# A hybrid decoder step: sampling attention with its first loads issued in the phase before, window keys laid in memory order, and the gate products moved in between each unit's keys and values

## The reference, cut to what matters

```python
# A: dilated window attention of the sampling rows over a cache, 3 head groups x 4 heads
sc = einsum('bqhe,bqjhe->bhqj', q, g[:, :, :, 0]) * e ** -0.5     # g: keys gathered by stride
p, den, lse = masked_softmax_parts(sc, valid)
# B: forgetting attention of the sampling rows over paged keys and values, 8 heads, 2048 past rows
s_past = einsum('bqhe,bkhe->bhqk', q, k_past) * e ** -0.5 + cq - c_past
# both row groups: the merge of the branches, gated
mix = (sigmoid(h @ w_ga) * (o_a @ w_pa) + sigmoid(h @ w_gb) * (o_b @ w_pb)) @ w_o
```

## Time and profile before

| | |
|---|---|
| median of 3 runs | 1196.73 us (1194.1 to 1200.82) |
| the profiled execution: its own time, its span | 1199.27 us, 1197.5 us |
| PE busy, DVE busy, ACT busy in the span | 1000.1, 379.9, 206.0 us |
| phase C: first scores to first product of phase D | 397.4 to 794.4 us |
| PE busy in phase C | 323.8 of 397.0 us |
| phase B's second to fifth key loads and last modulation weights: issued from, last weights used | 343.3, 386 us |

### The profile page before, as it was taken

The page is one execution under the profiler, slowest core; times in us unless marked ns, Lnnn a source line. Parts: engine busy times, 40 slices in busy tenths (PEclk is TensorE's granted clock), DMA queues, the critical chain, the costliest instruction groups (busy, mean ns, idle before and its releaser), DMA issues. The chain is left out here.

```text
span 1197.5 us, 17987 instructions
## 1 busy us (share of the span) xinstructions
PE 1000.1 (84%) x7324; PEld 585.3 (49%) x7324; DVE 379.9 (32%) x865; ACT 206.0 (17%) x509; POOL 187.3 (16%) x210
## 2 busy tenths in 40 slices
PE   3999999997897169979989997579977998777770
PEld 2444444444564046647656674136554554444430
DVE  3100033237751164516701771003451222100105
ACT  3000000014542011100020003001231211111114
POOL 0000033311200100022222311100003322212110
PEclk9999999999997589989989998669978999989995
DMA  9976666977787779998969984979187999999966
GB/s 339 355 278 248 249 248 248 326 244 255 256 212 168 207 240 213 289 349 322 370 231 334 364 320 151 391 266 341 57 325 269 364 370 383 379 393 394 397 256 237
DMA packets 98062, 348.48 MB, mean 291 GB/s; under 512 B 13018, under 2 KB 56802, under 8 KB 78654
## 3 DMA queue, kind: packets, MB, share of 16 engines
q1 hardware_dynamic: 80478, 265.90, 64.8%
q0 software_dynamic: 15552, 79.97, 18.1%
q10 hardware_dynamic: 1952, 1.48, 0.5%
HBM read 335.46 MB, written 63.36 MB: 333 GB/s over the span
## 5 line engine op out<-in xcount | busy, mean ns | idle before, releaser
L1605 PE MATMUL bank<-turned,w_all 128*128 128x320 f32 (+1 forms) x512 | 143.7, 425 | 0.0
L442 PE MATMUL bank<-w_all,turned 128*128 128x481 f32 (+2 forms) x384 | 119.3, 503 | 1.1 <-DVE turned L651 1.1
L442 PE MATMUL bank<-w_ring,turned 128*128 128x481 f32 (+2 forms) x384 | 118.4, 502 | 0.0
L2013 PE MATMUL bank<-w_all,mix_row 128*64 128x256 f32 x736 | 92.2, 407 | 26.9 <-DMA w_all<-in_w_exp 25.8
L1605 PEld LDWEIGHTS bank<-turned,w_all 128*128 128x128 f32 x512 | 95.3, 196 | 35.6 <-issue 15.5
L2013 PEld LDWEIGHTS bank<-w_all,mix_row 128*64 128x64 f32 x736 | 60.9, 147 | 65.3 <-issue 46.4
L1709 DVE STREAM_TRANSPOSE mods<-w_all 128x2048 f32<-128x2048 f32 (+1 forms) x39 | 86.6, 2239 | 9.8 <-PE bank L1481 7.1
L442 PEld LDWEIGHTS bank<-w_all,turned 128*128 128x128 f32 (+1 forms) x384 | 56.8, 171 | 61.5 <-issue 58.3
L442 PEld LDWEIGHTS bank<-w_ring,turned 128*128 128x128 f32 (+1 forms) x384 | 57.1, 171 | 60.4 <-issue 57.3
L2059 DVE COPY act_t<-bank 128x128 f32<-128x128 f32 x33 | 9.6, 292 | 200.8 <-PE bank L2023 199.1
L661 DVE COPY w_all<-bank 128x481 f32 (+5 forms) x32 | 16.9, 531 | 152.6 <-PE bank L442 152.4
(11 more groups left out here) (357 smaller groups left out, 1318.5 us busy)
## 6 DMA issues: line engine op xcount, KB each, us to landing
w_all<-in_w_exp SPq DMA_DIRECT2D x22, 2048.0 KB, 41.0
out_a_sample<-in_cache_a SPq DMA_DIRECT2D x8, 4080.0 KB, 21.4
w_all<-in_w_exp SPq DMA_DIRECT2D x25, 1024.0 KB, 39.2
mods<-in_w_ada SPq DMA_DIRECT2D x21, 1024.0 KB, 8.8
w_all<-in_cache_a SPq DMA_DIRECT2D x96, 128.0 KB, 7.5
w_all<-in_cache_a SPq DMA_DIRECT2D x40, 256.0 KB, 6.1
turned<-in_w_exp SPq DMA_DIRECT2D x5, 2048.0 KB, 42.2
mods<-in_w_exp SPq DMA_DIRECT2D x5, 2048.0 KB, 43.7
```

The costliest lines, as they stand in the source:

```text
L442: mm = nc.tensor.matmul(m.banks[i][r:r + ROWS[i], 0:hi - lo], m.hT[:, k, i * P:i * P + ROWS[i]], ring[u][:, CW * k + lo:CW * k + hi], star ...
L1605: mm = nc.tensor.matmul(GATE[:, 0:WIDTH[h]], gate_w[b][k][:, c % 2 * P:(c % 2 + 1) * P], m.hT[:, k, 256 * h:256 * h + WIDTH[h]], start=k = ...
L2013: mm = nc.tensor.matmul(m.banks[2 + p][x * SLOTS:(x + 1) * SLOTS, 0:HID], hgT[:, k, :], m.weights(u)[:, (2 * k + x) * HID:(2 * k + x + 1) ...
```

## The change

It has six parts.

1. Window keys come as one transfer over 128 partitions and 1 KB pieces in memory order (key 4i+c on partition i) where there were four over 32 partitions (key 32c+i): 2 issues in place of 8 for a step, the same bytes and piece size.
2. `add_bias` reads the bank with a stride to put the scores back in key order; for that it takes 256 columns at a time, so a chunk is two operations where it was one.
3. The mask (now built with 128 rows, one transfer), the first gate weights (2 MB) and the first merge weights (0.75 MB) are issued by SP in phase B. The weights lie in slices of 6 rather than 7 per tile, which keeps clear of columns that phase B still reads.
4. The 8 tables of rows are computed by DVE in step 7, not ahead of step 1; the constants are waited for at chunk 3.
5. `TURN = 5` pieces stand in front of the first value step of each unit and `LATE = 2` behind the last key step, so 7 in each handover; the other 52 are spread over steps 1 to 87 at 0.63 per step.
6. ACT takes the tangents of these in the same places, one of them between the two exponentials of kind "b"; the copies of the mixed rows (`LAST_PIECE + 2`) move from step 81 to 89.

```diff
-    for j in range(4):
-        src = I[name][4 * u + j].rearrange("(c i t) n -> i t c n", c=4, t=t)[:, t0:t0 + n, :, 0:AH * HD]
-        dst = slot[32 * j:32 * j + 32, 0:n * 4 * AH * HD].rearrange("p (t c n) -> p t c n", t=n, c=4)
-        for x in range(n):
-            eng.dma_start(dst[:, x], src[:, x]).then_inc(arrived, 16)
+    src = I[name][4 * u:4 * u + 4].rearrange("s (i c t) n -> (s i) t c n", c=4, t=t)[:, t0:t0 + n, :, 0:AH * HD]
+    dst = slot[:, 0:n * 4 * AH * HD].rearrange("p (c t n) -> p t c n", t=n, c=4)
+    for x in range(n):
+        eng.dma_start(dst[:, x], src[:, x]).then_inc(arrived, 16)
...
                 early_keys(k)
                 piece(BEFORE + 1 + k)
+                if k == 2:
+                    sp.dma_start(m.wmask, I["mask_window"]).then_inc(m.mask_in, 16)
+                    sp.wait_ge(turn_a, len(turns))
+                    sp.wait_ge(turn_d, len(turns))
+                    gate_weights_in(sp, I, m, 0, 0)
+                if k == 3:
+                    gate_weights_in(sp, I, m, 0, 1)
+            merge_weights_in(sp, I, m, 0)
...
-    FIRST, END = 3, 80
-    piece_at = {}
-    for n, x in enumerate(pieces):
-        piece_at.setdefault(FIRST + n * (END - FIRST) // len(pieces), []).append(x)
+    LATE, TURN, END = 2, 5, 88
+    first_v = [at[(u, "v", 0)] for u in range(len(UNITS))]
+    rate = (len(pieces) - len(UNITS) * (LATE + TURN)) / (END - 1 - len(UNITS))
+    piece_at, late_at, todo, due = {}, {}, list(pieces), 0.0
+    for t in range(1, N):
+        due += 0 if t in first_v else rate
+        count = TURN if t in first_v else min(int(due + 1e-6), len(todo))
+        due -= 0 if t in first_v else count
+        piece_at[t], todo = todo[:count], todo[count:]
+        if t + 1 in first_v:
+            late_at[t], todo = todo[:LATE], todo[LATE:]
...
-                    cols = slice(512 * c, 512 * c + (512 if c < 3 else P))
-                    ins = add(sc_a[:, cols], S(u, c)[:, 0:cols.stop - cols.start], wmask[:, cols], peak[:, 0, c:c + 1])
+                    dve.wait_ge(m.mask_in, 16)
                     if c == 3:
-                        ins = add(sc_a[:, AT * P:AT * P + GROUPS * NS], S(u, c)[:, P:P + GROUPS * NS], mask_a[:, own(u), :], peak[:, 0, 4:5])
+                        dve.wait_ge(con_in, 16)
+                    for g in (2 * c, 2 * c + 1) if c < 3 else (6,):
+                        lo, w = g % 2 * 256, P if g == 6 else 256
+                        by_key = lambda x: x.rearrange("p (y c) -> p y c", c=4)
+                        ins = add(by_key(sc_a[:, 256 * g:256 * g + w]), S(u, c)[:, lo:lo + w].rearrange("p (c y) -> p y c", c=4),
+                                  by_key(wmask[:, 256 * g:256 * g + w]), peak[:, 0, g:g + 1])
...
-                for x in piece_at.get(t, []):
-                    if x in sums:
-                        gates(*x)
+                now = [x for x in piece_at.get(t, []) if x in sums]
+                for x in now[1:] if t in first_v and kind(STEPS[t][0]) == "b" else now:
+                    gates(*x)
...
             turn(0)
-            dve.wait_ge(pages_in, 16 * 2)
-            for j in range(4):
-                rows = slice(32 * j, 32 * j + 32)
...
-            dve.wait_ge(con_in, 16 * 5)
...
+                    if (u, part, g) == (0, "v", 0):
+                        rows_of_pages()
```

More of the change, by code:

```diff
@@ L129, in build @@
         m.wp_in, m.wo_in = [ctx.enter_context(nc.semaphore(n)) for n in ("w_p", "w_o")]
+        m.gate_in = [ctx.enter_context(nc.semaphore(f"gate_w{b}")) for b in range(2)]
+        m.merge_in, m.mask_in = [ctx.enter_context(nc.semaphore(n)) for n in ("merge_w", "mask_rows")]
         with ExitStack() as attn:
@@ L214, in constants @@
             "over_ids": np.arange(EXPERTS, BLOCKS, dtype=np.float32)[None, :],
-            "mask_window": np.concatenate(window, axis=1), "sample_consts": sample_consts,
+            "mask_window": np.tile(np.concatenate(window, axis=1), (4, 1)), "sample_consts": sample_consts,
             "page_consts": np.concatenate([before, seq_of, tri8], axis=1),
@@ L1177, in phase_c @@
         filled = from_pages if kind(u) == "b" else from_window
-        filled[slot_of[n]] += 16 * (1 if kind(u) == "b" else 8 if part == "k" and g < 6 else 4)
+        filled[slot_of[n]] += 16 * (1 if kind(u) == "b" else 4 if part == "v" else 2 if g < 6 else 1)
         level.append(filled[slot_of[n]])
@@ L1232, in phase_c @@
             pieces += [("gate", c, h, 1, 0), ("gate", c, h, 1, 4), ("out", c, h, 0, 0)]
-    FIRST, END = 3, 80
-    piece_at = {}
-    for n, x in enumerate(pieces):
-        piece_at.setdefault(FIRST + n * (END - FIRST) // len(pieces), []).append(x)
-    step_of = {x: t for t, xs in piece_at.items() for x in xs}
+    LATE, TURN, END = 2, 5, 88
[9 more added lines that the diff above has]
+            late_at[t], todo = todo[:LATE], todo[LATE:]
+    assert not todo
+    step_of = {x: t for xs in (piece_at, late_at) for t, ys in xs.items() for x in ys}
+    LAST_PIECE = max(step_of.values())
     items = [x[1:3] for x in pieces if x[0] == "out"]
@@ L1296, in phase_c @@
         bias_in = [sem(f"bias{x}") for x in range(4)]
-        gate_in, wp_in = [sem(f"gate_w{b}") for b in range(2)], sem("merge_w")
+        gate_in, wp_in = m.gate_in, m.merge_in
         gain_in, terms, terms_out = sem("gains"), sem("terms"), sem("terms_out")
@@ L1617, in _ @@
                     (score if STEPS[t][1] == "k" else weigh)(t)
+                for x in late_at.get(t, []):
+                    piece(*x)
                 for x in use_at.get((t, "after"), []):
@@ L1656, in gates, with exps @@
                 ins.then_inc(th_ok, 1)
-            def exps(u):
+            def exps(u, between):
                 for h in range(1 if kind(u) == "a" else 2):
+                    if h:
+                        for x in between:
+                            gates(*x)
                     e = u if kind(u) == "a" else 2 + 2 * own(u) + h
@@ L1687, in _ @@
                 if t + 1 < N and STEPS[t][1] == "k" and STEPS[t + 1][1] == "v":
-                    exps(STEPS[t][0])
-                if t == max(piece_at) + 2:
+                    for x in late_at[t]:
+                        if x in sums:
+                            gates(*x)
+                    exps(STEPS[t][0], [x for x in piece_at[t + 1] if x in sums][:1])
+                if t == LAST_PIECE + 2:
                     act.wait_ge(mixed, 2 * KD)
@@ L1739, in maxima @@
                 for h in range(1 if kind(u) == "a" else 2):
-                    V.tensor_reduce(nm[:, h:h + 1], peak[:, h, :], AX, ALU.max, negate=True).then_inc(mx, 1)
+                    V.tensor_reduce(nm[:, h:h + 1], peak[:, h, 0:8 if kind(u) == "a" else 5], AX, ALU.max, negate=True).then_inc(mx, 1)
             def recips(u):
@@ L1852, in _ @@
                         recips(u)
+                for x in late_at.get(t, []):
+                    if x[0] == "out":
+                        mixing(*x[1:3])
                 for x in use_at.get((t, "after"), []):
```

60 lines of the change are left out of this document (32 added, 28 removed).

## The result

The changed kernel takes **1164.26 us** in the median of 4 runs (1160.8 to 1167.1), the kernel before 1196.7 beside it: ratio 0.9725, 95% interval 0.9681 to 0.9768. Forecast were 1161 us and 1147 to 1177. The profiled execution took 1167.1 us (span 1165.2), 3 above the median.

What follows compares the result with a forecast made beforehand. Phase C was taken as bound mostly by PE's list of steps and pieces, plus a 27.70 us first stall. Stretches summed to 361.8 against 397.0 us; with 4 gained in phase B and 3 given back, 1161 us, range 1147 to 1177.

Steps and rivals of the forecast that it cites:

- First stretch: Start of phase C: the 27.7 us wait goes, DVE is late next, 48.2 us becomes 20.
- Handovers: From a unit's keys to its values: seven pieces cover the exponentials, with tangent waits 19 us each.
- Key steps: PE waits for DVE, so less is saved than the pieces removed: unit 1 19 us, unit 2 51, unit 3 48.
- unit 3's keys: Key steps of unit 3 in phase C, with two `out` pieces instead of four: 48 us, before 53.2.
- transfers that collide in kind "b": Loads competing from step 28 to 59, 104 us of loads in 115 us: 3 us given back in the sum.
- Tail: Unit 3's values to phase D: 29.3 and 52.7 us; phase D 28 us after w_o goes out, or 38.
- rival (d): End of phase C: w_o load late in full, 10 us, and strided addings cost; 1172 us, chance 0.07.
- Rival (c): DVE keeps ahead of PE in key steps (41.5, not 49) and w_o lands early; 1147 us, chance 0.14.
- Phase B: Faster key loads remove the 4.12 us wait for a modulation weight: 4 us gain, bounds plus 4 and minus 8.
- Rival (b): Key loads stay at 225 GB/s; unit 1's keys and phase B's last weights late; 1176 us, chance 0.15.
- The rule against the change: Key loads: 512 KiB pitch per partition slows copies to 207 GB/s; here 128 KiB, so loads might stay near 225.
- Rival (e): Phase C: transfers set the pace and stop 19 us in each handover; not faster, 1210 us, chance 0.04.

Runs made afterwards that it cites:

- e5: Changed kernel with keys still in memory order, but each step loaded by four pairs of transfers onto 32 partitions: ratio 0.9931, 1189.1 us.
- e10: Changed kernel with the bias loads ahead of the gate and merge weights in SP's list, at their old steps: 1154.4 us, ratio 0.9641.
- e3: Changed kernel with END = 80 in place of 88, so the spread pieces end at step 79: 1159.2 us, ratio 0.9629.
- e4: Changed kernel with the bias loads ahead of the weights in SP's list, third and fourth part a step earlier: 1147.9 us, ratio 0.9557.
- e8: e4 with two pieces in place of five before each first value step, so four in a handover, not seven: 1145.6 us, ratio 0.9566.
- e11: Repetition of e8 on one chip with e10 and e12: 1142.3 us, ratio 0.9562.
- e2: Changed kernel with the old key loads, key order and single adding of 512 columns put back: 1188.5 us, ratio 0.9894.
- e6: Kernel before the change with only the tables moved to step 7 and the constants waited for at the first mask adding: 1183.6 us, ratio 0.9889.
- e7: Changed kernel with the eight tables put back in front of step 1's keys in DVE's list: 1167.9 us, ratio 0.9788.
- e1: Changed kernel with gate and merge pieces spread as before over steps 3 to 79, none gathered in handovers: 1152.9 us, ratio 0.9602.
- e12: Repetition of e1 on one chip with e10 and e11: 1154.4 us, ratio 0.9655.

## Why the prediction was right, point by point

The range held and the sum was 3 us low. That is closer than the steps deserve, since two errors offset each other.

- **First stretch,** forecast 20, measured 16.2. The mechanism held: DVE is busy 14.5 of 16.2 us. The strided addings cost what was taken, 0.41 us each.
- **Handovers,** forecast 19, measured 17.5. The term was over-sized by the tangent's price: 0.56 to 0.68, not the 0.8 to 0.9 that I took from a copy's wait. Unit 0's, 1's and 2's stretches with them came to 38.6, 34.7 and 64.3 (39.8, 37 and 65).
- **Key steps.** Unit 1: 22.4 for 19, with waits for DVE of 1.2 and 2.9 us that the walk did not have; the longer one is the late `c_pages` (see e5). Unit 2: 53.4 for 51, with three waits (1.2, 2.5, 2.6) behind DVE's turns and not the 8 to 10 us named. The window's clock was 0.87, which the walk did not have either.
- **The step that failed: unit 3's keys,** forecast 48, measured 61.7. I walked PE, DVE and the slots, and did not walk SP's list through steps 61 to 75, where the new spread brought gate and merge weights to the very steps of the bias. I had written of transfers that collide in kind "b" and given 3 us for it in the sum; the collision was 12.7 us in one place. Without it the stretch is 49. In e10 only the order in SP's list was changed and this wait is gone, so the weights in front are what made it. In e3 the bias is late without them, so they are not all of it; the gathers are the likely rest, which no run shows.
- **Tail,** 77.9 for 82.0: w_o after step 87 and phase D 26.4 us later, where 28 (and at most 38) stood. My lower value was right; rival (d) did not come about. The first values of phase C came 22.7 us earlier, not the 30 named as a sign: the handover's seven pieces stand ahead of them.
- **Sum.** 361.8 plus 3 was forecast, 369.2 came. Less the stall's surplus it would be about 357, and e4 (357.0) and e10 (355.3) measured that. So the sum was some 5 to 9 us high everywhere else, and the missed stall hid it: that the total came out 3 us off is luck. Rival (c), more than I sum, is what e8 and e11 reach.
- **Phase B,** forecast 4 us earlier, measured 3.8. In the ten executions with the same lists up to there phase C starts between 388.0 and 395.6 us, 391.8 in the mean (397.4 before): 5.6, with a scatter as large as the effect. The reason given was that the wait for a modulation weight goes. It is 1.37 us in the changed kernel, but 4.0 to 4.7 in six of the ten (4.12 before), which is the sign named for being wrong. So the size came out and the mechanism is not shown.
- **Rival (b),** slow keys, did not come, but e5 and e2 show its price. It had phase B's last weights 8 us late, and e5's phase C starts 8.1 us after the 397.4 of before. It had unit 1's keys 6 us late; e5 waits 11.0 us there where the changed kernel waits 2.9, so 8, but for `c_pages` and not for keys: the size was near, the path was wrong. The profiled executions are 15.6 us apart (span 1180.8 against 1165.2; forecast were 15), of which 11.8 are the start of phase C; the phase itself is only 2.4 us longer, since the bias costs PE 7.3 us there and 12.7 here. By the ratios it is 25: the profiled execution is the fastest of e5's eight and the slowest of the changed kernel's four.
- **The rule against the change** (the Trainium skill, DMA: Bandwidth & Descriptors, "Latency and other measured facts", copies slowed at a pitch of 512 KiB) had no effect at the 128 KiB here: the window with 368 GB/s holds loads of steps 3 and 4, which have it (it is in the third to sixth step of a unit, not in one alone). This section of the Trainium skill has 207 GB/s at 512 KiB against 214 as the full rate of such copies, both between tensors in HBM, so it spoke against the change less than the prediction has it. The section "Rules for kernel authors" on the same page of the Trainium skill, one transfer over 128 partitions, is what e5 bears out.
- **Rival (e),** transfers that stop in the handovers, exists: share 0.00 from 684 to 702 us, 0.01 from 570 to 578. It did not decide, since in units 0 and 1 the share stays at 0.86 and 0.79 over handover and values. Four pieces in place of seven win 7 to 9 us of the phase, in line with it; that the stops alone are their price is not shown.
- **The gain's parts.** Of 32 us the keys' layout is 20 (e2). The tables' move alone is worth 13 us (e6), and 4 to 7.5 on top of the rest of the change (e7, intervals that overlap); the early loads were not measured alone, and the parts do not add up. The placing of pieces, the part with the largest diff, cost 0.7 to 1.3% as made (e1, e12).

The best version is the changed kernel with the bias first and four pieces in a handover: 1142.3 us, 0.9562, 1.7% under the changed one (e4, with seven, has 0.9557 on another chip).

## What to carry to other kernels

When pieces of work move, walk the queue of their transfers too: a small load that a bank or a buffer waits for belongs ahead of megabytes that are due later, above all where another queue fills the engines. Two of the waits here were of this kind, the bias behind weights and `c_pages` behind keys, and the second was at first read as a wait for the keys: follow a wait through every engine down to a transfer before you name it. A stall that ends at one late item often has the next one right behind it: ask for each change alone what is late then, as e6 and e7 do. Filler work between two dependent parts is worth as much as the wait that it covers, and four pieces covered nearly all of it here; with seven (e10) little more was covered and the transfers stood still longer than with four (e11), some 12 us for 10 in unit 3's handover and 6 for 3 in unit 2's.

## What was not expected of the hardware

- With POOL's gathers outstanding, SP's queue got 19.2% of the engines, 58 GB/s, and a bias of 0.25 MB took 28 us to land; SP's own issue of one such load took 11.1 us, and 0.5 at the shortest of the same four.
- Packets of the same size took an engine 81 ns in the mean in loads partly over 32 partitions and 61 ns over 128, at a DMA share above 1 in both: a share near 1 does not say that the transfers run at their best rate.
- With equal lists up to there, ten kernels began phase C anywhere between 388.0 and 395.6 us. The wait for the last modulation weights (1.3 to 4.7 us) does not order them: with 1.31 us e1 began at 388.0 and with 1.37 us the changed kernel at 393.6, 5 us behind it already ahead of that wait. What sets the scatter is open.
